# Token gates as one rounded product per token, with two pairs of PSUM banks, and the gated units unpaired

## Chip, core and metric

One NeuronCore of a Trainium2 chip runs the whole program. The metric is the device time of one execution in microseconds; before the change the median of three runs is 1869.54 us (1869.54 to 1873.31).

## What is computed

The program is a transformer of two blocks for 256 tokens of width 1024, in float32. The change lies in the last part of the second block, a retrieval of single-neuron experts. Each token has 8 heads, each head picks 16 of 128 x 128 = 16,384 experts, and each picked expert has a gate (a softmax over the 16 scores):

```
experts, gates = top 16 per head of s1[i1] + s2[i2], expert = i1 * 128 + i2
u = u_tab[ec]
a = gelu(einsum('td,thkd->thk', hc, u))
out = einsum('thk,thkd->td', gc * a, v_tab[ec])
```

The kernel does not gather. It computes h . u for all 16,384 experts and all tokens, applies gelu, multiplies by a dense matrix of gates that is zero for the experts not picked, and multiplies the result with the whole of v_tab.

## The kernel before

SyncE streams the weights through a ring of four units of 128 x 1024 floats. Float32 accuracy is had by splitting: ScalarE rounds a unit to fp32r (`ring_hi`, `unit_hi`, L489), GpSimd or VectorE computes the rest (`ring_lo`, `unit_lo`, L495), and TensorE adds the three products hi x hi, hi x lo and lo x hi. Every engine has its own queue, worked off in the order in which the code issues it, and they meet only in semaphores: `full[b]` says that TensorE has filled PSUM bank b, `emptied[b]` that it may be filled again.

The stage "peer_u" has 128 units, one per value of i2. A unit gives a tile of 128 experts (i1, on the partitions) x 256 tokens, in bank 4 or 5 in turn. There are two ways to compute it. `h_tile` (L541) issues 24 matmuls of 256 columns (L550). `h_pair_tile` (L557) puts the high and low part of h side by side as 512 columns: 8 matmuls of 512 (L562) and 8 of 256 (L568), after which the two halves of the bank must be added.

The first 44 units (`h_tile`) run while VectorE still searches the top 16. Then it hands over three rows per token: i1, i2 and the gate, 128 picks on the partitions, 256 tokens in the free dimension. From there on the 84 *gated* units run, and between them the gates are made, in 64 groups of four tokens, four groups in five units. For a token, the 128 x 128 gate matrix is the product of two one-hot matrices over the 128 picks: `hot1` (pick x i1) and `hot2` (pick x i2, multiplied by the gate). So before unit k, for its group g:

- VectorE (`one_hots`) makes `hot2` and `hot1` for four tokens with two comparisons against an iota row in PSUM and multiplies `hot2` by the gate (L2727, L2728, L2730). There are two buffers, one in the tile `late`, one over unused constants in `cst`; group g+2 is made when group g has been multiplied.
- TensorE (`token_gates`, L1264) computes four f32 products of 128 columns into one of three banks 0 to 2.
- VectorE (`gate_tokens`) multiplies the gelus of the units done so far by the gates (L2737) and copies the gates of the units to come into the places of their gelus in `act_e`, inside the tile `arena` (L2738). The n units done and the 128 - n others always make 4 x 128 elements.

For each unit VectorE adds the two halves of the pair into bank 6 or 7 (`unit_sum`, L2771), ScalarE applies gelu there (L1822; the tokens that have no gate yet go straight to `act_e`, L1824), and VectorE multiplies by the gates that are there (`gate_unit`, L2750), one unit later. After the 84 units comes the product with v_tab (L615).

Of the kernel before, what the change touches and what calls it, by code (L numbers as in the profile page):

```python
# [25 lines left out]
ALU = mybir.AluOpType  # L26
# [3 lines left out]
P = 128  # L30
# [18 lines left out]
HOT_BANKS = 3  # L49
# [163 lines left out]
def build(nc, stream, x_t, x_rows, ctx_t, params, consts, decay, lam_in, rel_bias, onehot, dist_mask, scale_w, aside_w, c_rows, ln_rows,  # L213
          bias_rows, gate_cols, out):
    with ExitStack() as ctx:
# [11 lines left out]
        def sem(name):  # L227
            return ctx.enter_context(nc.semaphore(name))
# [27 lines left out]
        gate_r = rounded("gate_r", "gate_lo", [P, T])  # L256
        e_pair = rounded("e_pair", "late", [P, 4, 2 * T], 2048)
# [33 lines left out]
        def h_parts(like, skip):  # L291
# [70 lines left out]
        hot1, hot2 = ([a[:, at:at + 4 * P].rearrange("p (t e) -> p t e", t=4) for a, at in places] for places in (  # L362
            ((late, 2048), (cst, CONST["cos_2d"])), ((late, 3072), (cst, CONST["mean_64"]))))
# [22 lines left out]
        iota_ps = ps[:, 3, 0:P]  # L386
        gate_ps = ps[:, 3, P:P + T]
# [7 lines left out]
        iota16_ps = ps[:, 7, 0:TOPK]  # L395

# [78 lines left out]
        unit_gelu = sem("unit_gelu")  # L475
# [25 lines left out]
        def _(pe):  # L501
# [733 lines left out]
            def peer_u_pair(n):  # L1235
                h_pair_tile(FIRST_UNIT["peer_u"] + n, h_parts_3, h_hi_3, 4 + n % 2)

# [20 lines left out]
            def token_gates(g):  # L1258

                b = g % HOT_BANKS  # L1260
                pe.wait_ge(hot_ready, g + 1)
                start_fill(b)
                for t in range(4):
                    m = pe.matmul(ps[:, b, t * P:(t + 1) * P], hot1[g % 2][:, t, :], hot2[g % 2][:, t, :], start=True, stop=True)  # L1264
                m.then_inc(full[b], 1)
                fills[b].add()

            for k in range(GATED_UNITS):
                for g in groups_before(k):
                    token_gates(g)  # L1270
                peer_u_pair(FIRST_GATED + k)
# [36 lines left out]
        def _(act):  # L1308
# [506 lines left out]
            for k in range(GATED_UNITS):  # L1815
                n = FIRST_GATED + k
                b = 4 + n % 2
                t = tokens_gated(k)
                unit_hi(act, FIRST_UNIT["peer_u"] + n + 2)
                act.wait_ge(emptied[b], drains[b].add())  # L1820
                total = ps[:, 6 + k % 2, 0:T]
                m = act.activation(total[:, 0:t], total[:, 0:t], ACT.Gelu)  # L1822
                if t < T:
                    m = act.activation(act_e[:, n, t:T], total[:, t:T], ACT.Gelu)  # L1824
                m.then_inc(unit_gelu, 1)
                if k >= GATED_UNITS - 3:
                    expert_hi(k - (GATED_UNITS - 3))
# [14 lines left out]
        def _(dve):  # L1842
# [877 lines left out]

            def one_hots(g):

                def of_tokens(a):
                    return a[:, 4 * g:4 * g + 4].unsqueeze(2).broadcast_to([P, 4, P])

                iotas = spread(iota_ps, 4)
                step(dve.tensor_tensor(hot2[g % 2], iotas, of_tokens(i2_t), ALU.is_equal))  # L2727
                dve.tensor_tensor(hot1[g % 2], iotas, of_tokens(i1_t), ALU.is_equal)  # L2728
                settle()
                dve.tensor_tensor(hot2[g % 2], hot2[g % 2], of_tokens(gate_ps), ALU.mult).then_inc(hot_ready, 1)  # L2730

            def gate_tokens(g, units):

                b = g % HOT_BANKS
                gates = ps[:, b, :].rearrange("p (t e) -> p e t", t=4)
                a = act_e[:, :, 4 * g:4 * g + 4]
                dve.tensor_tensor(a[:, 0:units], a[:, 0:units], gates[:, 0:units], ALU.mult)  # L2737
                dve.tensor_copy(a[:, units:N_EXP], gates[:, units:N_EXP]).then_inc(emptied[b], 1)  # L2738
# [4 lines left out]
            def gate_unit(k):  # L2743

                n = FIRST_GATED + k
                t = tokens_gated(k)
                dve.wait_ge(unit_gelu, k + 1)
                last_group = t // 4 - 1
                dve.wait_ge(emptied[last_group % HOT_BANKS], reads[last_group % HOT_BANKS].n)
                dve.tensor_tensor(act_e[:, n, 0:t], ps[:, 6 + k % 2, 0:t], act_e[:, n, 0:t],  # L2750
                                  ALU.mult).then_inc(unit_gated, 1)

            for g in range(2):
                one_hots(g)
# [11 lines left out]
            def unit_sum(k):  # L2766

                n = FIRST_GATED + k
                b = 4 + n % 2
                dve.wait_ge(full[b], n_u[n % 2].add())  # L2770
                dve.tensor_reduce(ps[:, 6 + k % 2, 0:T], ps[:, b, :].rearrange("p (a t) -> p t a", a=2), AX_X,  # L2771
                                  ALU.add).then_inc(emptied[b], 1)

            for k in range(GATED_UNITS):
                for g in groups_before(k):
                    filled(g % HOT_BANKS)
                    if g + 2 < GROUPS:
                        one_hots(g + 2)
                    if k >= 1:
                        dve.wait_ge(unit_gelu, k)  # L2780
                    gate_tokens(g, FIRST_GATED + k)
                if k >= 1:
# [4 lines left out]
            gate_unit(GATED_UNITS - 1)  # L2787
# [294 lines left out]
```

## Time and profile before

| | |
|---|---|
| median of three runs | 1869.54 us |
| the profiled execution, its own time | 1871.33 us |
| its span in the profile | 1869.5 us |
| TensorE busy | 97% |
| VectorE / GpSimd / ScalarE busy | 68% / 53% / 46% |
| granted TensorE clock, mean | 0.99 |

The busy share of TensorE is a sum over instructions that overlap, with modelled ends; how much time they really take is read from the distance between starts. The gated stage runs from 1224.0 us (first token product) to 1516.7 (first product of experts). A tile is named as the trace names it: `ps` is PSUM, `h_span` the split h, `late`, `cst` and `arena` are tiles in SBUF.

### The profile page before, as it was taken

How to read it: one execution, taken by the hardware profiler on the slowest of the kernel's cores; microseconds unless marked ns; L12 is line 12 of the kernel's file. 1: busy time of each engine (PE TensorE's matmuls, PEld its weight loads, DVE VectorE, ACT ScalarE, POOL GpSimd, SP SyncE). 2: the span in 40 equal slices, each digit the busy share in tenths (PEclk: the TensorE clock that was granted, in tenths of full speed). 3: DMA queues.
4: the chain of work that ended last, by engine and by line, in shares of the span. 5: the costliest groups of instructions: out<-in, count | busy, mean ns of one | idle time of the engine just before them, and what ended most of it. 6: DMA issues, size and time to landing. Idle time of an engine off the chain costs nothing.

```text
span 1869.5 us, 29721 instructions
## 1 busy us (share of the span) xinstructions
PE 1809.0 (97%) x10462; PEld 1528.3 (82%) x10462; DVE 1265.2 (68%) x2109; ACT 850.7 (46%) x1379; POOL 998.1 (53%) x431
## 2 busy tenths in 40 slices
PE   5999889998999999999999999999999999999999
PEld 1847579987978887788978899989988988888887
DVE  6587757888548777433233379978888867777776
ACT  3033545445445554542453546643343345554454
POOL 4034046443675543775438768876666654444443
PEclk7999999999999999999999999999999999999999
DMA  8787236886665554552325455544444455555555
GB/s 321 254 305 254 76 126 235 283 275 216 205 212 176 189 189 160 176 167 102 114 90 170 158 180 180 181 148 149 154 147 148 156 181 192 192 196 194 191 191 168
DMA packets 95316, 345.93 MB, mean 185 GB/s; under 512 B 10544, under 2 KB 12032, under 8 KB 94592
## 3 DMA queue, kind: packets, MB, share of 16 engines
q1 hardware_dynamic: 78048, 283.67, 45.1%
q10 hardware_dynamic: 17184, 61.11, 9.4%
q8 instruction: 56, 0.92, 0.2%
q14 instruction: 28, 0.23, 0.0%
HBM read 343.66 MB, written 1.08 MB: 184 GB/s over the span
## 4 chain that ended last, share of the span: by engine, by line
PE 87%; DVE 5%; DMA 3%; ACT 2%; POOL 1%; issue 1%; ACTq 0%; DVEq 0%; SPq 0%
PE ps L615 29%; PE ps L550 18%; PE ps L562 14%; PE ps L568 7%; PE ps L1264 3%; PE ps L771 2%; PE ps L534 2%; PE ps L685 2%; PE ps L838 2%; DMA ring<-stream 2%; PE ps L1001 1%; POOL ring_lo L495 1%; PE ps L785 1%; DMA cst<-consts 1%; PE ps L595 1%
## 5 line engine op out<-in xcount | busy, mean ns | idle before, releaser
L495 POOL TENSOR_TENSOR ring_lo<-ring,ring_hi 128x1024 fp32r<-128x1024 f32 x371 | 898.0, 2426 | 683.0 <-ACT ring_hi L489 681.5
L489 ACT ACTIVATE ring_hi<-ring 128x1024 fp32r<-128x1024 f32 x502 | 531.7, 1060 | 487.3 <-DMA ring<-stream 483.4
L562 PE MATMUL ps<-h_span,ring_hi 128*128 128x512 f32 x1120 | 286.0, 397 | 0.0
L550 PE MATMUL ps<-h_span,ring_hi 128*128 128x256 f32 x1952 | 258.1, 285 | 0.1
L615 PE MATMUL ps<-ring_hi,e_pair 128*128 128x512 f32 x1024 | 253.7, 389 | 1.0 <-DVE e_pair L2761 1.0
L550 PEld LDWEIGHTS ps<-h_span,ring_hi 128*128 128x128 f32 x1952 | 245.3, 192 | 5.7 <-issue 3.1
L2761 DVE TENSOR_TENSOR e_pair<-arena,e_pair 128x256 fp32r<-128x256 f32 x128 | 174.8, 1367 | 99.7 <-ACT e_pair L1813 99.3
L562 PEld LDWEIGHTS ps<-h_span,ring_hi 128*128 128x128 f32 x1120 | 202.6, 189 | 38.1
L615 PEld LDWEIGHTS ps<-ring_hi,e_pair 128*128 128x128 f32 x1024 | 192.0, 188 | 41.2 <-issue 1.4
L495 DVE TENSOR_TENSOR ring_lo<-ring,ring_hi 128x1024 fp32r<-128x1024 f32 x141 | 176.6, 1253 | 37.2 <-ACT ring_hi L489 36.9
L615 PE MATMUL ps<-ring_hi,arena_r 128*128 128x512 f32 x672 | 175.6, 394 | 2.3 <-ACT ring_hi L489 2.3
L568 PEld LDWEIGHTS ps<-h_span,ring_lo 128*128 128x128 f32 x1120 | 152.6, 190 | 11.8 <-POOL ring_lo L495 0.3
L568 PE MATMUL ps<-h_span,ring_lo 128*128 128x256 f32 x1120 | 156.0, 282 | 0.0
L2368 DVE CAST arena_r<-arena 128x256 fp32r<-128x256 f32 x64 | 105.2, 1644 | 70.0 <-ACT arena L1634 35.2
L615 PEld LDWEIGHTS ps<-ring_hi,arena_r 128*128 128x128 f32 x672 | 123.0, 190 | 26.4 <-ACT ring_hi L489 2.8
L550 PE MATMUL ps<-h_span,ring_lo 128*128 128x256 f32 x976 | 137.9, 284 | 0.3 <-POOL ring_lo L495 0.3
L615 PE MATMUL ps<-ring_lo,e_pair 128*128 128x512 f32 x512 | 137.5, 389 | 0.0
L550 PEld LDWEIGHTS ps<-h_span,ring_lo 128*128 128x128 f32 x976 | 126.7, 193 | 0.7 <-POOL ring_lo L495 0.7
L615 PEld LDWEIGHTS ps<-ring_lo,e_pair 128*128 128x128 f32 x512 | 96.1, 188 | 20.0
L1822 ACT ACTIVATE ps<-ps 128x256 f32<-128x256 f32 (+39 forms) x84 | 22.7, 270 | 173.3 <-DVE ps L2771 173.3
L615 PE MATMUL ps<-ring_lo,arena_r 128*128 128x512 f32 x320 | 91.8, 394 | 5.0 <-POOL ring_lo L495 2.8
L2352 DVE TENSOR_REDUCE arena<-ps 128x256 f32<-128x512 f32 x56 | 38.5, 687 | 65.6 <-PE ps L568 65.6
(292 smaller groups left out, 2249.4 us busy)
## 6 DMA issues: line engine op xcount, KB each, us to landing
ring<-stream SPq DMA_DIRECT2D x540, 512.0 KB, 3.3
arena<-aside_w ACTq DMA_DIRECT2D x49, 512.0 KB, 4.7
late<-aside_w ACTq DMA_DIRECT2D x21, 512.0 KB, 4.6
resid<-aside_w ACTq DMA_DIRECT2D x10, 512.0 KB, 6.4
arena<-scale_w ACTq DMA_DIRECT2D x8, 512.0 KB, 15.5
arena<-ln_rows ACTq DMA_DIRECT2D x8, 512.0 KB, 5.0
arena<-gate_cols ACTq DMA_DIRECT2D x2, 1024.0 KB, 5.0
arena<-decay ACTq DMA_DIRECT2D x1, 1536.0 KB, 6.8
```

The costliest lines, as they stand in the source:

```text
L489: act.activation(ring_hi[:, s, :], ring[:, s, :], ACT.Copy).then_inc(hi_ready, 1)
L495: eng.tensor_tensor(ring_lo[:, s, :], ring[:, s, :], ring_hi[:, s, :], ALU.subtract).then_inc(lo_ready[s], 1)
L534: m = pe.matmul(ps[:, bank, at:at + n], w[:, kc * P:(kc + 1) * P], r, start=kc == 0, stop=kc == KC - 1)
L550: m = pe.matmul(ps[:, bank, 0:T], w[:, kc * P:(kc + 1) * P], x[:, kc, :], start=begin, stop=w is w_lo and kc == KC - 1)
L562: m = pe.matmul(ps[:, bank, :], w_hi[:, kc * P:(kc + 1) * P], parts[kc], start=kc == 0, stop=False, skip_group_check=True)
L568: m = pe.matmul(ps[:, bank, 0:T], w_lo[:, kc * P:(kc + 1) * P], h_hi[:, kc, :], start=False, stop=kc == KC - 1, skip_group_check=True)
L615: m = pe.matmul(ps[:, b, :], x[:, tt * P:(tt + 1) * P], w[:, half * 512:(half + 1) * 512], start=start, stop=stop, skip_group_check=True)
L685: pe.matmul(shape, lhs, rhs, start=True, stop=True).then_inc(full[bank], 1)
L1264: m = pe.matmul(ps[:, b, t * P:(t + 1) * P], hot1[g % 2][:, t, :], hot2[g % 2][:, t, :], start=True, stop=True)
L2352: dve.tensor_reduce(dst, ps[:, b, :].rearrange("p (a t) -> p t a", a=2), AX_X, ALU.add).then_inc(emptied[b], 1)
L2368: dve.tensor_copy(hid_hi[:, j % 4, :], hid2[:, j % 4, :]).then_inc(hid_hi_ready, 1)
L2761: dve.tensor_tensor(e_lo[:, e % 4, :], act_e[:, e if row is None else row, :], e_hi[:, e % 4, :], ALU.subtract).then_inc(e_lo_ready, 1)
```

## The change

The gates are now split like everything else. The gate is rounded to fp32r (`gate_hi`), the rest is `gate_lo`, and VectorE makes a `hot2` of 256 columns per token, hi part and lo part side by side, both fp32r; TensorE multiplies it in one fp32r matmul of 256 columns. A group of four tokens now fills two banks, 0 and 1 or 2 and 3, in turn. The two halves of the result have to be added: ScalarE copies the hi half out of PSUM (for the n units done to one of two new buffers `gate_part`, for the others into `act_e`), and VectorE adds the lo half to both and then multiplies the first sum by the gelus. The gated units go through `h_tile` instead of `h_pair_tile`, so their sum is complete in bank 4 or 5, `unit_sum` goes, gelu reads that bank and writes to bank 6, and `gate_unit` comes in the same turn of the loop. Iota and gates move to bank 7, the gates for half of the tokens at a time.

```
-HOT_BANKS = 3
+HOT_BANKS = ((0, 1), (2, 3))
...
             def token_gates(g):
-                b = g % HOT_BANKS
                 pe.wait_ge(hot_ready, g + 1)
-                start_fill(b)
-                for t in range(4):
-                    m = pe.matmul(ps[:, b, t * P:(t + 1) * P], hot1[g % 2][:, t, :], hot2[g % 2][:, t, :], start=True, stop=True)
-                m.then_inc(full[b], 1)
-                fills[b].add()
+                for first, b in zip((0, 2), HOT_BANKS[g % 2]):
+                    start_fill(b)
+                    for t in range(2):
+                        m = pe.matmul(ps[:, b, t * T:(t + 1) * T], hot1[g % 2][:, first + t, :],
+                                      hot2_parts[g % 2][:, first + t, :], start=True, stop=True)
+                    m.then_inc(full[b], 1)
+                    fills[b].add()
...
-                peer_u_pair(FIRST_GATED + k)
+                peer_u_tile(FIRST_GATED + k)
...
                 unit_hi(act, FIRST_UNIT["peer_u"] + n + 2)
-                act.wait_ge(emptied[b], drains[b].add())
-                total = ps[:, 6 + k % 2, 0:T]
-                m = act.activation(total[:, 0:t], total[:, 0:t], ACT.Gelu)
+                for g in groups_before(k):
+                    low, high = HOT_BANKS[g % 2]
+                    act.wait_ge(full[low], mark["group", g][low])
+                    act.wait_ge(full[high], mark["group", g][high])
+                    if g >= 2:
+                        act.wait_ge(emptied[low], mark["group", g - 2][low])
+                    hi, _, tokens, part = group_parts(g)
+                    act.activation(part[:, 0:n], hi[:, 0:n], ACT.Copy)
+                    act.activation(tokens[:, n:N_EXP], hi[:, n:N_EXP], ACT.Copy).then_inc(group_copied, 1)
+                act.wait_ge(full[b], drains[b].add())
+                if k >= 1:
+                    act.wait_ge(unit_gated, k)
+                m = act.activation(gelu_ps[k % 2][:, 0:t], ps[:, b, 0:t], ACT.Gelu)
                 if t < T:
-                    m = act.activation(act_e[:, n, t:T], total[:, t:T], ACT.Gelu)
-                m.then_inc(unit_gelu, 1)
+                    m = act.activation(act_e[:, n, t:T], ps[:, b, t:T], ACT.Gelu)
+                m.then_inc(emptied[b], 1)
...
-            step(dve.tensor_copy(gate_hi[:, :], ps[:, 6, 0:T]))
+            step(dve.tensor_copy(gate_r[:, :], ps[:, 6, 0:T]))
             settle()
-            dve.tensor_copy(gate_ps, gate_hi[:, :]).then_inc(emptied[6], 1)
+            step(dve.tensor_copy(gate_hi[:, :], gate_r[:, :]))
+            settle()
+            dve.tensor_tensor(gate_lo[:, :], ps[:, 6, 0:T], gate_hi[:, :], ALU.subtract).then_inc(emptied[6], 1)
...
+            def half_gates(tt):
+                c = slice(tt * P, (tt + 1) * P)
+                dve.tensor_copy(gate_hi_ps, gate_hi[:, c])
+                step(dve.tensor_copy(gate_lo_ps, gate_lo[:, c]))
...
-                step(dve.tensor_tensor(hot2[g % 2], iotas, of_tokens(i2_t), ALU.is_equal))
-                dve.tensor_tensor(hot1[g % 2], iotas, of_tokens(i1_t), ALU.is_equal)
+                hi, lo = hot2_parts[g % 2][:, :, 0:P], hot2_parts[g % 2][:, :, P:2 * P]
+                step(dve.tensor_tensor(hi, iotas, of_tokens(i2_t), ALU.is_equal))
+                dve.tensor_tensor(hot1[g % 2][:, :, :], iotas, of_tokens(i1_t), ALU.is_equal)
                 settle()
-                dve.tensor_tensor(hot2[g % 2], hot2[g % 2], of_tokens(gate_ps), ALU.mult).then_inc(hot_ready, 1)
+                dve.tensor_tensor(lo, hi, of_tokens(gate_lo_ps, 4 * g % P), ALU.mult)
+                dve.tensor_tensor(hi, hi, of_tokens(gate_hi_ps, 4 * g % P), ALU.mult).then_inc(hot_ready, 1)
...
-                dve.tensor_tensor(a[:, 0:units], a[:, 0:units], gates[:, 0:units], ALU.mult)
-                dve.tensor_copy(a[:, units:N_EXP], gates[:, units:N_EXP]).then_inc(emptied[b], 1)
+                low, high = HOT_BANKS[g % 2]
+                dve.wait_ge(group_copied, g + 1)
+                hi, lo, a, part = group_parts(g)
+                step(dve.tensor_tensor(hi[:, 0:units], lo[:, 0:units], part[:, 0:units], ALU.add))
+                dve.tensor_tensor(a[:, units:N_EXP], lo[:, units:N_EXP], a[:, units:N_EXP], ALU.add)
+                settle()
+                dve.tensor_tensor(a[:, 0:units], hi[:, 0:units], a[:, 0:units], ALU.mult).then_inc(emptied[low], 1)
+                dve.wait_ge(emptied[low], mark["group", g][low])
+                dve.sem_inc(emptied[high], 1)
...
             for k in range(GATED_UNITS):
                 for g in groups_before(k):
...
-                if k >= 1:
-                    gate_unit(k - 1)
-                unit_sum(k)
+                gate_unit(k)
```

On TensorE, this is the second group and the second gated unit, before the change (`hot_ready` counts one-hots made; an f32 product stands here as one instruction and in the trace as two):

```order
L1264 MATMUL ps<-cst 128x128 [waits emptied1,hot_ready]
L1264 MATMUL ps<-cst 128x128 x3
L562 MATMUL ps<-h_span_52,ring_hi 128x512 [waits emptied5,hi_ready]
L562 MATMUL ps<-h_span_52,ring_hi 128x512 x7
L568 MATMUL ps<-h_span_52,ring_lo_49 128x256 [waits lo_ready1]
L568 MATMUL ps<-h_span_52,ring_lo_49 128x256 x7
```

and with it:

```order
L1270 MATMUL ps<-hot2_parts_b_55,hot1_b_57 128x256 [waits emptied2,hot_ready]
L1270 MATMUL ps<-hot2_parts_b_55,hot1_b_57 128x256
L1270 MATMUL ps<-hot2_parts_b_55,hot1_b_57 128x256 [waits emptied3]
L1270 MATMUL ps<-hot2_parts_b_55,hot1_b_57 128x256
L559 MATMUL ps<-h_span_52,ring_hi 128x256 [waits emptied5,hi_ready]
L559 MATMUL ps<-h_span_52,ring_hi 128x256 x15
L559 MATMUL ps<-h_span_52,ring_lo_49 128x256 [waits lo_ready1]
L559 MATMUL ps<-h_span_52,ring_lo_49 128x256 x7
```

The four products wait for two banks instead of one and are twice as wide; the unit's 8 + 8 matmuls have become 24.

On VectorE, one turn of the loop with a group, before the change: the one-hots, the gates of the tokens, the gated unit of the turn before, the sum of the halves.

```order
L2727 TENSOR_TENSOR cst<-ps,late 128x512 [waits full1]
L2728 TENSOR_TENSOR cst<-ps,late 128x512
L2730 TENSOR_TENSOR cst<-cst,ps 128x512 [waits dve_step]
L2737 TENSOR_TENSOR arena<-arena,ps 128x45x4 [waits unit_gelu]
L2738 COPY arena<-ps 128x83x4
L2750 TENSOR_TENSOR arena<-ps,arena 128x4 [waits emptied0,unit_gelu]
L2771 TENSOR_REDUCE ps<-ps 128x256 [waits full5]
```

and with it:

```order
L2754 TENSOR_TENSOR hot2_parts_b_55<-ps,late 128x4x128 [waits full3,full2]
L2755 TENSOR_TENSOR hot1_b_57<-ps,late 128x512
L2757 TENSOR_TENSOR hot2_parts_b_55<-hot2_parts_b_55,ps 128x4x128 [waits dve_step]
L2758 TENSOR_TENSOR hot2_parts_b_55<-hot2_parts_b_55,ps 128x4x128
L2765 TENSOR_TENSOR ps<-ps,gate_part_b 128x45x4 [waits group_copied]
L2766 TENSOR_TENSOR arena<-ps,arena 128x83x4
L2768 TENSOR_TENSOR arena<-ps,arena 128x45x4 [waits dve_step]
L2783 TENSOR_TENSOR arena<-ps,arena 128x8 [waits emptied2,emptied5]
```

`hot2_parts_b` and `hot1_b` are the second buffer of one-hots. There is a fourth operation on the one-hots, the copy has become an addition and one more addition stands ahead of the multiply, which waits for the first addition (`dve_step`). The wait for ScalarE's copies (`group_copied`) is new. The row of `gate_unit` now ends the turn of its own unit, waiting for that unit's gelu (`emptied5`), and the reduce is gone.

On VectorE ahead of the first group, from the last of the three handed-over rows to the first one-hots, before the change:

```order
L2713 COPY gate_hi<-ps 128x256 [waits full6]
L2715 COPY ps<-gate_hi 128x256 [waits dve_step]
L2717 COPY ps<-cst 128x128 [waits emptied7]
L2727 TENSOR_TENSOR late<-ps,late 128x512 [waits emptied6,iota_ready]
L2728 TENSOR_TENSOR late<-ps,late 128x512
L2730 TENSOR_TENSOR late<-late,ps 128x512 [waits dve_step]
```

and with it:

```order
L2731 CAST gate_r_53<-ps 128x256 [waits full6]
L2733 CAST gate_hi<-gate_r_53 128x256 [waits dve_step]
L2735 TENSOR_TENSOR gate_lo<-ps,gate_hi 128x256 [waits dve_step]
L2737 COPY ps<-cst 128x128 [waits emptied7]
L2744 COPY ps<-gate_hi 128x128 [waits emptied6,iota_ready]
L2745 COPY ps<-gate_lo 128x128
L2754 TENSOR_TENSOR hot2_parts_a_54<-ps,late 128x4x128 [waits dve_step]
L2755 TENSOR_TENSOR hot1_a_56<-ps,late 128x512
L2757 TENSOR_TENSOR hot2_parts_a_54<-hot2_parts_a_54,ps 128x4x128 [waits dve_step]
L2758 TENSOR_TENSOR hot2_parts_a_54<-hot2_parts_a_54,ps 128x4x128
```

A cast and a subtraction are new, and the gates are copied to PSUM as two halves of 128 columns, ahead of four instead of three operations on the one-hots.

## Rows read from the trace of the kernel before

**Rows 1.** The page: busy us (share of span) of each engine; TensorE clock in slices.

```profile
PE 1809.0 (97%) x10462; PEld 1528.3 (82%) x10462; DVE 1265.2 (68%) x2109; ACT 850.7 (46%) x1379; POOL 998.1 (53%) x431
...
PEclk7999999999999999999999999999999999999999
```

**Rows 2.** Busy us (x instructions) of each engine in the gated stage.

```profile
1224.00:1516.70 292.70, 292.70 (x1858) 263.30 (x1857) 237.42 (x482) 117.02 (x248) 197.26 (x83) 1.00 0.46 151
```

**Rows 3.** Timeline of TensorE: start us, us, engine, line, operation, tiles, count.

```profile
1302.62 2.09 PE L562 MATMUL ps<-h_span,ring_hi 128*128 128x512 f32 x8
...
1305.50 1.05 PE L1264 MATMUL ps<-cst 128*128 128x128 f32 x8
1306.31 0.96 PE L562 MATMUL ps<-h_span,ring_hi 128*128 128x512 f32 x3
```

**Rows 4.** Timeline of TensorE at the end of the stage, units without a group.

```profile
1505.53 2.00 PE L562 MATMUL ps<-h_span,ring_hi 128*128 128x512 f32 x8
...
1508.32 2.00 PE L562 MATMUL ps<-h_span,ring_hi 128*128 128x512 f32 x8
```

**Rows 5.** Timeline of TensorE in the stage just before, unpaired units.

```profile
1193.55 2.08 PE L550 MATMUL ps<-h_span,ring_hi 128*128 128x256 f32 x16
...
1196.43 2.08 PE L550 MATMUL ps<-h_span,ring_hi 128*128 128x256 f32 x16
```

**Rows 6.** Timeline of VectorE beside rows 3.

```profile
1302.90 0.69 DVE L2727 TENSOR_TENSOR late<-ps,late 128x512 f32<-128x512 f32 x1 [0.19 <-PE ps L1264]
1303.51 0.68 DVE L2728 TENSOR_TENSOR late<-ps,late 128x512 f32<-128x512 f32 x1
1304.11 0.68 DVE L2730 TENSOR_TENSOR late<-late,ps 128x512 f32<-128x512 f32 x1
1304.70 0.42 DVE L2737 TENSOR_TENSOR arena<-arena,ps 128x264 f32<-128x264 f32 x1
1305.04 0.41 DVE L2738 COPY arena<-ps 128x248 f32<-128x248 f32 x1
1305.37 0.22 DVE L2750 TENSOR_TENSOR arena<-ps,arena 128x72 f32<-128x72 f32 x1
1305.70 0.70 DVE L2771 TENSOR_REDUCE ps<-ps 128x256 f32<-128x512 f32 x1
```

**Rows 7.** Timeline of VectorE late in the stage.

```profile
1490.83 0.65 DVE L2737 TENSOR_TENSOR arena<-arena,ps 128x476 f32<-128x476 f32 x1
1491.39 0.19 DVE L2738 COPY arena<-ps 128x36 f32<-128x36 f32 x1
1491.49 0.40 DVE L2750 TENSOR_TENSOR arena<-ps,arena 128x240 f32<-128x240 f32 x1
```

**Rows 8.** Timeline of ScalarE beside rows 3, and the split behind the gelu.

```profile
1302.74 0.21 ACT L1822 ACTIVATE ps<-ps 128x72 f32<-128x72 f32 x1 [2.32 <-DVE ps L2771]
1302.87 0.32 ACT L1824 ACTIVATE arena<-ps 128x184 f32<-128x184 f32 x1
1303.07 1.06 ACT L489 ACTIVATE ring_hi<-ring 128x1024 fp32r<-128x1024 f32 x1
```

**Rows 9.** Timeline of VectorE before the first group.

```profile
1214.61 2.31 DVE L2706 TENSOR_TENSOR cst<-cst,small 128x128 f32<-128x128 f32 x1
...
1218.48 0.42 DVE L2713 COPY gate_hi<-ps 128x256 f32<-128x256 f32 x1 [0.20 <-PE ps L1251]
1218.93 0.43 DVE L2715 COPY ps<-gate_hi 128x256 f32<-128x256 f32 x1
...
1220.80 0.68 DVE L2730 TENSOR_TENSOR late<-late,ps 128x512 f32<-128x512 f32 x1
```

**Rows 10.** Timeline of GpSimd over the same stretch.

```profile
1214.36 2.41 POOL L495 TENSOR_TENSOR ring_lo<-ring,ring_hi 128x1024 fp32r<-128x1024 f32 x1 [2.08 <-ACT ring_hi L489]
1217.00 4.76 POOL L495 TENSOR_TENSOR ring_lo<-ring,ring_hi 128x1024 fp32r<-128x1024 f32 x2 [0.23 <-ACT ring_hi L489]
```

**Rows 11.** Timeline of TensorE at the first group.

```profile
1224.04 1.06 PE L1264 MATMUL ps<-late 128*128 128x128 f32 x8
```

More of the change, by code:

```diff
@@ L256, in build @@
         gate_r = rounded("gate_r", "gate_lo", [P, T])
+        hot2_parts = [rounded("hot2_parts_a", "late", [P, 4, 2 * P], 2048), rounded("hot2_parts_b", "cst", [P, 4, 2 * P], CONST["cos_2d"])]
+        hot1 = [rounded("hot1_a", "late", [P, 4, P], 3072), rounded("hot1_b", "cst", [P, 4, P], CONST["mean_64"])]
+        gate_part = [sb("gate_part_a", [P, N_EXP - 4, 4]), sb("gate_part_b", [P, N_EXP - 4, 4])]
         e_pair = rounded("e_pair", "late", [P, 4, 2 * T], 2048)
@@ L395, in build, with group_parts @@
         iota16_ps = ps[:, 7, 0:TOPK]
+        gelu_ps = [ps[:, 6, 0:T], ps[:, 6, T:2 * T]]
+        def group_parts(g):
+            low = HOT_BANKS[g % 2][0]
+            parts = ps[:, low:low + 2, :].rearrange("p b (t a e) -> p e (b t) a", t=2, a=2)
+            return parts[:, :, :, 0], parts[:, :, :, 1], act_e[:, :, 4 * g:4 * g + 4], gate_part[g % 2]
         landed = [sem(f"landed{s}") for s in range(RING)]
@@ L1258, in token_gates @@
             def token_gates(g):
-                b = g % HOT_BANKS
                 pe.wait_ge(hot_ready, g + 1)
-                start_fill(b)
-                for t in range(4):
-                    m = pe.matmul(ps[:, b, t * P:(t + 1) * P], hot1[g % 2][:, t, :], hot2[g % 2][:, t, :], start=True, stop=True)
-                m.then_inc(full[b], 1)
-                fills[b].add()
+                for first, b in zip((0, 2), HOT_BANKS[g % 2]):
[5 more added lines that the diff above has]
+                    fills[b].add()
+                mark["group", g] = [fills[b].n for b in range(4)]
             for k in range(GATED_UNITS):
@@ L2764, in expert_lo @@
                     unit_lo(dve, FIRST_UNIT["peer_v"] + e, i)
[L2766 to L2772, printed above, removed]
             for k in range(GATED_UNITS):
                 for g in groups_before(k):
-                    filled(g % HOT_BANKS)
+                    for b in HOT_BANKS[g % 2]:
+                        dve.wait_ge(full[b], mark["group", g][b])
+                    if g + 2 == GROUPS // 2:
+                        half_gates(1)
+                        settle()
                     if g + 2 < GROUPS:
                         one_hots(g + 2)
-                    if k >= 1:
-                        dve.wait_ge(unit_gelu, k)
                     gate_tokens(g, FIRST_GATED + k)
-                if k >= 1:
-                    gate_unit(k - 1)
-                unit_sum(k)
+                gate_unit(k)
                 if k >= GATED_UNITS - 3:
                     expert_lo(k - (GATED_UNITS - 3))
-            gate_unit(GATED_UNITS - 1)
             for e in range(3, 8):
```

26 lines of the change are left out of this document (11 added, 15 removed).

## Prediction

> **What bounds the kernel now.** I read the engine table first: TensorE is busy for 97% of the span and the granted clock stands at its 2.4 GHz level in every slice but the first [rows 1]. A reader should then ask which stage the change touches and whether TensorE has any idle time there. The table of windows, cut at the first and the last matmul of the gated stage, answers both: 292.7 us, TensorE busy in all of them, VectorE for 237.4, ScalarE for 117.0, GpSimd for 197.3, DMA under half [rows 2]. No engine makes TensorE wait there, so an edit that takes TensorE time out of this stage gives it back one for one, until another engine needs more than what is left. That engine would be VectorE, at 81% now.
>
> The timeline gives the stage's rhythm. A unit with a group of token gates comes round every 1306.31 - 1302.62 = 3.69 us [rows 3], one without a group every 1508.32 - 1505.53 = 2.79 [rows 4]. So a group costs 0.90 us of TensorE, although its own starts are only 0.81 apart: the first matmuls behind it come a little later. 64 groups and 84 units give 64 x 3.69 + 20 x 2.79 = 292.0, against 292.7 measured. The model holds.
>
> **TensorE, the token products.** An f32 product of 128 columns stands in the trace as two instructions, eight per group of four tokens, 0.90 / 8 = 0.11 us each. After the change a token is one rounded matmul of 256 columns. The stage just before has hundreds of these, with the same kind of weight load: 24 of them from 1193.55 to 1196.43, that is 2.88 us, 0.120 each [rows 5]. A group becomes 4 x 0.120 = 0.48. Gain 0.42 x 64 = 26.9 us. Bounds for one product: below, 0.101, the distance of the starts of one f32 instruction now ((1306.31 - 1305.50) / 8), which would bring 4.9 us more; above, the 0.225 that a token costs now, which would take back all 26.9. I take 0.120, the row of the same shape.
>
> **TensorE, units unpaired.** 16 matmuls (8 of 512, 8 of 256 columns) become 24 of 256. The paired unit costs 2.79, the unpaired 2.88 [rows 4, 5], both on weights out of the same ring and the same h. Cost 0.09 x 84 = 7.6 us. Nothing has to be guessed here.
>
> So TensorE alone needs 84 x 2.88 + 64 x 0.48 = 272.6 us for the stage: 20.0 less than the 292.7. In five units (four with a group) it needs 5 x 2.88 + 4 x 0.48 = 16.32 instead of 4 x 3.69 + 2.79 = 17.55.
>
> **VectorE, the edit's price.** Per group now: three operations of 512 elements, 0.60 us from start to start, then 0.34 and 0.33 for the multiply and the copy, and per unit the 0.60 reduce and the multiply of the gated unit [rows 6]. After: four of the 512 kind (2.40), two additions which together always have 512 elements (0.34 + 0.33 = 0.67), a multiply of 4n elements, a wait for that multiply's own end, a semaphore increment, and the unit's multiply. The multiply costs 0.34 at n = 66 [rows 6] and 0.56 at n = 119 [rows 7]. Its own end comes 0.65 - 0.56 = 0.09 after the next could have started, plus 0.03 to go on (0.42 us from 1218.48, next at 1218.93) [rows 9]; the increment I estimate at 0.05, since no row shows one. The unit's multiply is 0.22 long at 72 elements and 0.40 at 240 [rows 6, 7], less the 0.07 by which the next one overlaps it: 0.15 and 0.33. Sum for a unit with a group, D: 2.40 + 0.67 + 0.34 + 0.17 + 0.15 = 3.73 at n = 66 and 2.40 + 0.67 + 0.56 + 0.17 + 0.33 = 4.13 at n = 119. The reduce is gone; the unit without a group costs VectorE 0.33.
>
> VectorE keeps pace while 4 D + 0.33 is under 16.32, so while D is under 4.00. By the line through the two values D passes it at n = 102, the 58th of the 80 units among which the groups are spread; from there to the last D is over by 0.08 on average, x 4/5 x 22 = 1.4 us in all. This is lag, not yet a stall of TensorE. VectorE frees the banks of a group about 4.6 us after the unit ahead of it ended, TensorE asks for them two groups later, after 6.72. Some 2 us of lag are covered, of which the lag inside a block of five uses part. I charge 0.5 us. This is the weakest number of the forecast: each 0.1 us more per group moves the crossing 13 units forward, and the excess grows with the square of the units behind it (1.4, 3.7, 7.0, 11 us for 0, 0.1, 0.2, 0.3 more), of which about 1 is covered. On the other side nothing is to be had: VectorE can't make TensorE faster than its own 16.32. That there are ends this far apart is why I keep B and C below.
>
> A new dependency comes with it: VectorE now ends every unit by waiting for that unit's gelu. From the end of a unit to the gelu's end lie 0.20 until another engine starts on it (TensorE goes on at 1305.50, VectorE starts at 1305.70) and 0.45 for both pieces [rows 3, 6, 8]; in units with a group VectorE arrives later anyway, in the fifth it waits and starts the next group's work 0.95 after the unit's end. That is in the 0.33 and the 16.32 above. Queued behind the wait are the one-hots of group g+2, which TensorE wants 3 us after they are due.
>
> The Trainium skill has a rule against this change. "VectorE: DVE Perf Modes", section "The DRAIN you can't avoid", says that the next operation doesn't start until the pipe of the one before is empty. By durations (0.68 instead of 0.60 for each large one, the same 0.08 for the small ones) VectorE would set the stage. Here the trace disagrees for this very mix: starts 0.60 apart at durations of 0.68 [rows 6]. But one of the new operations writes PSUM with a stride and the multiply reads what it wrote, so I keep it as a rival.
>
> **ScalarE.** It gains two copies per group, together 512 elements. The gelu pieces take 0.21 for 72 and 0.32 for 184 elements and together 0.45 from the first start to the end [rows 8]; twice the elements, by the slope of these two rows ((0.32 - 0.21) / 112 = 1 ns each), make some 0.7 for both copies. Its load becomes 5 x (1.06 + 0.45) + 4 x 0.7 = 10.4 of 16.32. The copies stand behind the 1.06 split of a ring unit, which waits for its DMA; with 0.65 for the gelu and nothing for the DMA they end 2.4 us after the unit's end, VectorE wants them at 0.95 + 2.40 = 3.35. Covered by 0.95, which a late landing may use up now and then.
>
> **Start and end of the stage.** Before the first group VectorE gains a cast and a subtraction of 256 elements, two copies of 128 and a fourth one-hot operation: 0.45 + 0.34 + 0.5 + 0.6 less the 0.34 copy that goes, 1.55 us. The one-hots of group 0 were ready at 1220.80 + 0.68 = 1221.48, while TensorE came for them at 1224.04 [rows 9, 11]. Cover 2.5. The cast reads and writes SBUF only. The row to look at is L2706: 2.31 us for 128 elements, where 256 took 0.43 at 1218.93, and it ends 0.15 after GpSimd's pass of 2.41 from 1214.36; another pair of GpSimd passes runs from 1217.00 to 1221.76, right where the cast will stand [rows 9, 10]. Held until the first of them ends (1219.4, 0.45 late), group 0 is ready at 1221.48 + 1.55 + 0.45 = 1223.5, still in time; held for both, 2.4 later, at 1225.9, 1.8 us late. I take the first. (The Trainium skill, "GPSIMD Engine Reference", section "Specifications", says that the SBUF interfaces are shared with VectorE, and that an operation in a 2-port mode or with two SBUF inputs contends. By that rule, the trace agrees.) At the stage's end VectorE leaves one unit earlier than now; TensorE hardly waits there today, so nothing.
>
> **Sum.** 26.9 - 7.6 = 19.3 by the parts, 20.0 by the stage (292.7 - 272.6; the 0.7 is what the rhythm model leaves out, half of it taken); less 0.5 for the lag and nothing for the start: 19.2. Against the profiled execution, span 1869.5 and its own time 1871.33, that is a span of 1850.3 and 1852.1. The median of the runs, 1869.54, lies 1.8 under the profiled one, and my forecast is for the median: 1850.3.
>
> **Rivals.**
> A, the forecast: TensorE bounds, 1850 (1847 to 1853). 68%.
> B, VectorE falls behind in part: 0.1 to 0.3 us more per group than I sum, from strided PSUM writes, the wait on its own multiply and the increment, or copies of ScalarE that come late. For 0.2 more: 7.0 - 1 = 6 lost instead of 0.5, 1855.8; for 0.3: 10 lost, 1860. For it: VectorE is filled to (64 x 3.86 + 20 x 0.33) / 272.6 = 93%; against: every operand shape but the PSUM-written sum has a row. 19%.
> C, VectorE sets the stage, the slower side: every operation of a group costs its duration, 7 x 0.08 = 0.56 more. D is then 3.86 + 0.56 = 4.42 on average over n = 44 to 123, and the excess 64 x 0.42 = 27, less 1 covered, against 19.7 gained: 1876. It decides from a mean D of 4.32 on (64 x 0.32 = 20.5), 0.46 above mine. 8%.
> D, the product is not cheaper: 256 columns with one-hots as the loaded weights cost the 0.225 per token of now, so only the unpairing is left, +7.6: 1877. The rows of 256 columns speak against it. 3%.
> Between B and C lies a strip in which gain and loss cancel to within 3.7 us. 2%.
>
> A difference below 0.2% (3.7 us) can't be told from no change. Faster: A + B = 0.87; same 0.02; slower C + D = 0.11. The range must hold 0.8: all of A and most of B, 1847 to 1862; the lower end takes in a product somewhat under 0.120.
>
> **What would show it.** The stage from the first token product to the first expert product takes 273 us instead of 292.7; a group's starts lie 0.48 apart and a unit's 2.88; TensorE stays at 99 to 100% busy there. VectorE's busy share of the stage rises above 90%. If B, TensorE shows idle time before a token product or the unit behind it, put down to VectorE, in the last third of the stage and not in the first; if C, in all of it; if D, matmuls of 256 columns 0.2 us apart with TensorE still full. A late first group would show as idle time of 1 to 2 us at 1224. The forecast is wrong if TensorE is full and the stage still isn't 17 us shorter.

## Result and the profile after

| | before | with the change |
|---|---|---|
| median of 8 runs each | 1874.13 us (1869.54 to 1880.07) | 1862.92 us (1858.26 to 1867.15) |
| ratio, 95% interval | 1 | 0.9932 (0.9914 to 0.9950) |
| the profiled execution, span | 1869.5 | 1856.2 |
| gated stage, first token product to first product of experts | 292.7 | 279.9 |
| the rest of the span | 1576.9 | 1576.3 |

The ratio stands for 12.7 us less (9.3 to 16.1); the profiled executions differ by 13.3, of which the gated stage holds 12.8. The forecast was 19.2 less. The forecast was written for 1869.54, the median of the first three of the eight runs of the kernel before; the median of all eight is 1874.13. Applied to 1869.54, the ratio gives 1856.8 (1853.5 to 1860.2): inside the range of 1847 to 1862, 6.5 above the forecast, and outside the 1847 to 1853 of its main case. A second measurement of the same kernel, beside the experiments below, gave 0.9952 (0.9934 to 0.9970).

The stage in the table of windows, columns as in [rows 2]:

```profile
1223.66:1503.54 279.88, 274.75 (x2274) 272.67 (x2273) 246.75 (x531) 156.97 (x376) 199.45 (x84) 1.00 0.48 159
```

TensorE was busy without a gap before; now it lacks 5.1 us, and VectorE is busy for 88% of a shorter stage. On TensorE the early part of the stage has this rhythm (timeline):

```profile
1305.00 0.64 PE L1270 MATMUL ps<-hot_parts_a,hot_a 128*128 128x256 f32 x4
1305.48 2.08 PE L559 MATMUL ps<-h_span,ring_hi 128*128 128x256 f32 x16
1307.40 1.12 PE L559 MATMUL ps<-h_span,ring_lo 128*128 128x256 f32 x8
1308.36 0.63 PE L1270 MATMUL ps<-hot_parts_b,hot_b 128*128 128x256 f32 x4
```

A group is 1305.48 - 1305.00 = 0.48 us and a unit 1308.36 - 1305.48 = 2.88, against the 3.69 for both in [rows 3]. Late in the stage the token products come late:

```profile
1477.36 0.63 PE L1270 MATMUL ps<-hot_parts_b,hot_b 128*128 128x256 f32 x4
1477.82 2.07 PE L559 MATMUL ps<-h_span,ring_hi 128*128 128x256 f32 x16
1479.73 1.12 PE L559 MATMUL ps<-h_span,ring_lo 128*128 128x256 f32 x8
1481.44 0.71 PE L1270 MATMUL ps<-hot_parts_a,hot_a 128*128 128x256 f32 x4 [0.59 <-DVE arena L2768]
1481.99 2.08 PE L559 MATMUL ps<-h_span,ring_hi 128*128 128x256 f32 x16
...
1485.72 0.71 PE L1270 MATMUL ps<-hot_parts_b,hot_b 128*128 128x256 f32 x4 [0.70 <-DVE arena L2768]
```

From 1477.82 to 1481.99 the unit with its group takes 4.17 instead of 3.36, so 0.81 are lost, of which the wait shown is 0.59; that is why ten waits of 5.0 us go with a stage that is some 8 us too long. The wait before the product is put down to the multiply L2768 of VectorE, which frees the banks. The table of waits of the stage (who waited for whom: us, times, longest) adds the same wait as seen from the weight load, ScalarE's waits for VectorE, and VectorE's waits for itself and for ScalarE:

```profile
ACT ps L1840 <- DVE arena L2783: 65.1, 33, 2.9
...
DVE arena L2783 <- DVE arena L2768: 14.1, 64, 0.6
DVE arena L2783 <- ACT ps L1840: 9.7, 5, 2.5
DVE arena L2783 <- ACT arena L1842: 9.2, 15, 1.0
PEld ps L1270 <- issue: 7.0, 11, 0.9
PE ps L1270 <- DVE arena L2768: 5.0, 10, 0.7
```

All ten waits of TensorE lie behind 1380 us, so from the 49th of the 84 gated units on. The five waits of 9.7 us stand in the last five units, after the groups; the 15 of 9.2 us stand in the units without a group before those, twelve of them 0.57 long. (The changed kernel's lines are numbered anew: L1270 is the token product, L559 the unit; the trace calls `hot2_parts_a` and `hot1_a` `hot_parts_a` and `hot_a`.) What VectorE does in a turn, early (timeline, n = 45):

```profile
1228.88 0.69 DVE L2754 TENSOR_TENSOR hot_parts_b<-ps,late 128x512 fp32r<-128x512 f32 x1
...
1231.95 0.33 DVE L2768 TENSOR_TENSOR arena<-ps,arena 128x180 f32<-128x180 f32 x1
1232.49 0.17 DVE L2783 TENSOR_TENSOR arena<-ps,arena 128x8 f32<-128x8 f32 x1 [0.21 <-DVE arena L2768]
1232.60 0.69 DVE L2754 TENSOR_TENSOR hot_parts_a<-ps,late 128x512 fp32r<-128x512 f32 x1
```

and late (n = 117), in the last turn of a block of five with a group and the fifth without one, with ScalarE's gelu of the fifth unit under it:

```profile
1472.33 0.68 DVE L2754 TENSOR_TENSOR hot_parts_b<-ps,late 128x512 fp32r<-128x512 f32 x1
...
1474.71 0.65 DVE L2765 TENSOR_TENSOR ps<-ps,gate_part_b 128x468 f32<-128x468 f32 x1
1475.27 0.19 DVE L2766 TENSOR_TENSOR arena<-ps,arena 128x44 f32<-128x44 f32 x1
1475.40 0.65 DVE L2768 TENSOR_TENSOR arena<-ps,arena 128x468 f32<-128x468 f32 x1
1476.26 0.41 DVE L2783 TENSOR_TENSOR arena<-ps,arena 128x240 f32<-128x240 f32 x1 [0.21 <-DVE arena L2768]
1477.24 0.41 DVE L2783 TENSOR_TENSOR arena<-ps,arena 128x240 f32<-128x240 f32 x1 [0.57 <-ACT arena L1842]
1477.56 0.68 DVE L2754 TENSOR_TENSOR hot_parts_a<-ps,late 128x512 fp32r<-128x512 f32 x1
```

```profile
1476.76 0.35 ACT L1840 ACTIVATE ps<-ps 128x240 f32<-128x240 f32 x1 [2.86 <-DVE arena L2783]
1477.03 0.18 ACT L1842 ACTIVATE arena<-ps 128x16 f32<-128x16 f32 x1
```

Early a turn costs 1232.60 - 1228.88 = 3.72 us. Late it costs 1476.26 + 0.32 - 1472.33 = 4.25 (0.32 is what the unit's multiply takes from start to start, 1477.24 to 1477.56). Between the multiply L2768 and the unit's multiply L2783 lie 0.21 us in which VectorE waits for its own last result. And in the fifth unit VectorE stands still for 0.57 until ScalarE's gelu is done, although the unit was finished long before: that gelu had itself waited for VectorE's multiply of the unit before.

Ahead of the first group VectorE's rows now read, answering to [rows 9]:

```profile
1218.57 0.60 DVE L2733 COPY gate_hi<-gate_r 128x256 f32<-128x256 f32 x1
1219.21 0.42 DVE L2735 TENSOR_TENSOR gate_lo<-ps,gate_hi 128x256 f32<-128x256 f32 x1
1219.55 0.28 DVE L2737 COPY ps<-cst 128x128 f32<-128x128 f32 x1
...
1222.19 0.68 DVE L2758 TENSOR_TENSOR hot_parts_a<-hot_parts_a,ps 128x512 fp32r<-128x512 f32 x1
```

The cast between two SBUF tiles is L2733. GpSimd ran here too (4.79 us for two passes from 1216.64, the first of them over at about 1219.04), and the cast lasted until 1219.17, 0.60 us for 256 elements where the subtraction behind it took 0.42. That fits a cast held until GpSimd's first pass ended; no run takes GpSimd away to show it. The first one-hots were ready at 1222.87, TensorE came at 1223.66. Nothing was lost.

### The profile page after: what moved, and what is told of

Same layout as the page of the kernel before. It is cut to its first block, busy times and chain, and to the rows that moved or that the text cites. A ratio compares the mean times of both kernels' runs of the same rounds, so it can differ in the third digit from the quotient of the medians.

```text
span 1856.2 us, 31003 instructions
## 1 busy us (share of the span) xinstructions
PE 1790.4 (96%) x10878; PEld 1537.8 (83%) x10878; DVE 1275.7 (69%) x2158; ACT 889.7 (48%) x1507; POOL 1004.1 (54%) x431
## 4 chain that ended last, share of the span: by engine, by line
PE 70%; DVE 14%; issue 6%; POOL 4%; DMA 3%; ACT 2%; DVEq 0%; ACTq 0%; POOLq 0%; SPq 0%
PE ps L624 26%; PE ps L559 19%; PE ps L571 5%; POOL ring_lo L504 4%; PE ps L577 3%; PE ps L780 2%; PE ps L543 2%; DMA ring<-stream 2%; PE ps L847 2%; PE ps L694 2%; PE ps L1010 2%; PE ps L794 1%; DVE arena L2768 1%; DVE ps L2765 1%; DMA cst<-consts 1%
## 5 line engine op out<-in xcount | busy, mean ns | idle before, releaser
L559 PE MATMUL ps<-h_span,ring_hi 128*128 128x256 f32 x3296 | 431.8, 284 | 0.0
L559 PEld LDWEIGHTS ps<-h_span,ring_hi 128*128 128x128 f32 x3296 | 411.4, 191 | 5.4 <-issue 3.3
L559 PE MATMUL ps<-h_span,ring_lo 128*128 128x256 f32 x1648 | 231.4, 283 | 0.8 <-POOL ring_lo L504 0.7
L559 PEld LDWEIGHTS ps<-h_span,ring_lo 128*128 128x128 f32 x1648 | 212.5, 192 | 1.5 <-POOL ring_lo L504 1.5
L571 PE MATMUL ps<-h_span,ring_hi 128*128 128x512 f32 x448 | 111.4, 391 | 0.0
L571 PEld LDWEIGHTS ps<-h_span,ring_hi 128*128 128x128 f32 x448 | 82.3, 188 | 16.0
L1354 ACT ACTIVATE arena<-ps 128x256 f32<-128x256 f32 (+2 forms) x90 | 34.7, 387 | 101.1 <-PE ps L559 89.5
L624 PEld LDWEIGHTS ps<-ring_lo,arena_r 128*128 128x128 f32 x320 | 59.8, 190 | 19.9 <-POOL ring_lo L504 4.5
```

The costliest lines, as they stand in the source:

```text
L559: m = pe.matmul(ps[:, bank, 0:T], w[:, kc * P:(kc + 1) * P], x[:, kc, :], start=begin, stop=w is w_lo and kc == KC - 1)
L571: m = pe.matmul(ps[:, bank, :], w_hi[:, kc * P:(kc + 1) * P], parts[kc], start=kc == 0, stop=False, skip_group_check=True)
L624: m = pe.matmul(ps[:, b, :], x[:, tt * P:(tt + 1) * P], w[:, half * 512:(half + 1) * 512], start=start, stop=stop, skip_group_check=True)
```

## Experiments

Stage lengths are those of each kernel's profiled execution, from the first token product to the first product of experts; span less stage is everything else, which no experiment touches. It lies between 1575.6 and 1584.2 (the changed kernel alone: 1576.3 and 1584.2), so the small steps are read from the stage and the ratio only confirms them.

| kernel | stage | rest | ratio to before, 95% interval |
|---|---|---|---|
| the kernel before | 292.7 | 1576.9 | 1 |
| changed | 279.9 | 1576.3 | 0.9932 (0.9914 to 0.9950) |
| changed, once more | 280.4 | 1584.2 | 0.9952 (0.9934 to 0.9970) |
| gelu in place | 276.8 | 1576.6 | 0.9923 (0.9900 to 0.9945) |
| one release | 271.8 | 1579.7 | 0.9902 (0.9880 to 0.9924) |
| both | 272.0 | 1575.6 | 0.9902 (0.9880 to 0.9925) |
| less work for VectorE | 271.8 | 1576.4 | 0.9894 (0.9851 to 0.9936) |
| more work for VectorE | 317.3 | 1580.4 | 1.0155 (1.0121 to 1.0188) |
| before, units unpaired | 298.8 | 1579.6 | 1.0030 (1.0013 to 1.0047) |

**The changed kernel again**, on the chip on which gelu in place, one release and both were measured. The other three experiments ran on a second chip, each beside the kernel before.

> The changed kernel as it is, beside the others on the same chip: stage 279.9 us, 7.6 of it idle time and late starts before token products from the 46th gated unit on, ratio to the kernel before 0.993.

The stage came out at 280.4, with 5.4 us of waits of the products and 7.7 of the weight loads ahead of them, at 11 and 13 places, the first before the 44th gated unit (1372.18 us), where the first run has its first before the 49th. The ratio was 0.9952 where 0.993 had been expected; the two intervals overlap. In the profiled execution what lies outside the stage was 7.9 us longer than in the first run. Part of it are waits of TensorE for `ring_lo` from VectorE in earlier stages, 7.0 us against 0.9; the rest is not traced.

**Less work for VectorE.**

```
-                dve.tensor_tensor(lo, hi, of_tokens(gate_lo_ps, 4 * g % P), ALU.mult)
+                if g < 2:
+                    dve.tensor_tensor(lo, hi, of_tokens(gate_lo_ps, 4 * g % P), ALU.mult)
```

> The changed kernel, but the multiplication of the one-hots by the low part of the gates is left out from the third group on (the low half keeps what an earlier group left, so the gates are wrong there). It takes 0.60 us of VectorE per group away and touches no wait, bank or transfer. Theory (VectorE's time is what TensorE waits for): D is 3.64 at most, 4 x 3.64 + 0.98 = 15.5 under 16.3, so no wait of TensorE is left, stage 272.3. Rival (copies of ScalarE, ring landings, or the bank order hold TensorE up): stage stays over 278.

```profile
1222.20:1493.98 271.78, 271.78 (x2274) 271.78 (x2273) 210.38 (x469) 161.99 (x376) 199.81 (x84) 1.00 0.49 164
```

TensorE is busy for all of 271.8 us, at the value that 84 units of 2.88 and 64 groups of 0.48 make (272.6), to 0.8. One VectorE operation less per group, with all waits, banks, copies and transfers as they were, removes all of the loss. So the loss was VectorE's time, not late copies or landings.

**More work for VectorE.**

```
                 step(dve.tensor_tensor(hi, iotas, of_tokens(i2_t), ALU.is_equal))
+                step(dve.tensor_tensor(lo, iotas, of_tokens(i2_t), ALU.is_equal))
```

> The changed kernel with one more comparison of 512 elements per group on VectorE, whose result is overwritten: 0.60 us per group more. Theory: VectorE sets the whole stage, five units take 4 x (3.98 + 0.60) + 0.98 = 19.3 on average against TensorE's 16.3, so 16 x 19.3 plus the four last units less the lag covered at the end, about 318 us; that is the slope of 0.6 us per group over the changed kernel's 280, and slower than the kernel before by some 25. Rival: a stage of under 290 would mean that VectorE was not near its limit.

The stage came out at 317.3, within a microsecond of the expectation, and the rival's 290 is out. TensorE late in the stage (timeline):

```profile
1496.29 0.63 PE L1270 MATMUL ps<-hot_parts_b,hot_b 128*128 128x256 f32 x4
1497.34 2.15 PE L559 MATMUL ps<-h_span,ring_hi 128*128 128x256 f32 x16 [0.42 <-ACT arena L1842]
...
1501.97 0.71 PE L1270 MATMUL ps<-hot_parts_a,hot_a 128*128 128x256 f32 x4 [1.52 <-DVE arena L2769]
...
1506.80 0.71 PE L1270 MATMUL ps<-hot_parts_b,hot_b 128*128 128x256 f32 x4 [1.24 <-DVE arena L2769]
```

The unit at 1497.34 waits for ScalarE's gelu to free its bank, and 62 of the gelus waited for a multiply of VectorE in this stage. 64 x 0.60 = 38.4 us more work gave 37.4 us more time. From where the kernel stands, these 38 us of VectorE cost almost as much time, while the one taken away in the experiment before gave back only 8.1 of 62 x 0.60 = 37.2: TensorE's own time is met after that.

**Gelu in place**, which takes the chain between gelu and multiply apart. In the changed kernel both gelu buffers lie in bank 6, and ScalarE waits (`unit_gated`) until VectorE has read the last before it writes the next.

```
-                if k >= 1:
-                    act.wait_ge(unit_gated, k)
-                m = act.activation(gelu_ps[k % 2][:, 0:t], ps[:, b, 0:t], ACT.Gelu)
+                m = act.activation(ps[:, b, 0:t], ps[:, b, 0:t], ACT.Gelu)
...
-                m.then_inc(emptied[b], 1)
+                m.then_inc(unit_gelu, 1)
...
-                dve.wait_ge(emptied[4 + n % 2], n_u[n % 2].add())
+                dve.wait_ge(unit_gelu, k + 1)
...
-                dve.tensor_tensor(act_e[:, n, 0:t], gelu_ps[k % 2][:, 0:t], act_e[:, n, 0:t],
-                                  ALU.mult).then_inc(unit_gated, 1)
+                dve.tensor_tensor(act_e[:, n, 0:t], ps[:, 4 + n % 2, 0:t], act_e[:, n, 0:t],
+                                  ALU.mult).then_inc(emptied[4 + n % 2], 1)
```

> The changed kernel, but gelu is applied in place in bank 4 or 5, VectorE reads it there and frees the bank, and ScalarE no longer waits for VectorE's multiply of the unit before. Theory (VectorE sets the pace late in the stage; a unit with a group costs it 3.72 us early and 4.24 late, and the fifth unit 0.98 instead of 0.33, because gelu of unit k waits for the multiply of k-1 and the multiply of k for that gelu): the fifth unit falls to about 0.35, VectorE keeps pace with TensorE's 16.3 per five units up to D = 4.0 instead of 3.83, and of the 7.6 us that the stage lasts over its 272.3 some 2 to 3 are left: stage about 275, span about 1851. Rival (ScalarE's copies or late ring landings hold VectorE up, the chain through gelu is covered by lag): stage stays at 280, within 1 us.

```profile
1467.36 0.68 DVE L2754 TENSOR_TENSOR hot_parts_b<-ps,late 128x512 fp32r<-128x512 f32 x1
...
1470.42 0.65 DVE L2768 TENSOR_TENSOR arena<-ps,arena 128x468 f32<-128x468 f32 x1
1471.28 0.72 DVE L2783 TENSOR_TENSOR arena<-ps,arena 128x240 f32<-128x240 f32 x2 [0.21 <-ACT arena L1841]
1471.92 0.68 DVE L2754 TENSOR_TENSOR hot_parts_a<-ps,late 128x512 fp32r<-128x512 f32 x1
```

The two unit multiplies now stand together (x2) and the last turn of a block with its fifth unit takes 1471.92 - 1467.36 = 4.56 instead of 1477.56 - 1472.33 = 5.23. The chain was there and cost 0.67 per block, as the theory says. The stage fell by 3.1 (3.6 beside its own repeat), to 276.8, while 5 had been expected. The waits before token products are gone. A wait of another kind took their place: VectorE now frees the unit's bank, and late in the stage TensorE waits for that, behind the first group of a block:

```profile
1470.53 0.64 PE L1271 MATMUL ps<-hot_parts_a,hot_a 128*128 128x256 f32 x4
1471.84 2.15 PE L560 MATMUL ps<-h_span,ring_hi 128*128 128x256 f32 x16 [0.67 <-DVE arena L2783]
```

There are six such waits (2.7 us) and nine of the weight load (4.4 us), and the stage is 5.0 longer than the 271.8 of a full TensorE. How much of that VectorE's excess would have cost anyway, 2 to 3 by the expectation, and how much is due to the bank that now comes free later, no run separates.

**One release.** The two banks of a group share one pair of semaphores, and the unit's multiply waits for the second addition, not for the multiply in front of it.

```
-                dve.tensor_tensor(a[:, units:N_EXP], lo[:, units:N_EXP], a[:, units:N_EXP], ALU.add)
-                settle()
+                first_sum = steps.now()
+                step(dve.tensor_tensor(a[:, units:N_EXP], lo[:, units:N_EXP], a[:, units:N_EXP], ALU.add))
+                dve.wait_ge(dve_step, first_sum)
                 dve.tensor_tensor(a[:, 0:units], hi[:, 0:units], a[:, 0:units], ALU.mult).then_inc(emptied[low], 1)
-                dve.wait_ge(emptied[low], mark["group", g][low])
-                dve.sem_inc(emptied[high], 1)
+                mark["second_sum"] = steps.now()
...
-                b = HOT_BANKS[last_group % 2][0]
-                dve.wait_ge(emptied[b], mark["group", last_group][b])
+                dve.wait_ge(dve_step, mark["second_sum"])
```

TensorE signals and waits for the low bank's semaphores alone, and so do the waits of ScalarE and VectorE.

> The changed kernel, but the two banks of a group share one pair of semaphores, so that VectorE neither waits for its own last multiply nor increments a second semaphore, and the unit's multiply waits only for the second addition. Theory: D falls by 0.22 to 0.30 us, to 3.45 early and 3.95 late; the excess never gets past the 2 us of cover; no idle time of TensorE before a token product; stage 272.5, span about 1848.7. Rival (what stalls is the order in which banks come free, two groups ahead, not VectorE's time): the release comes 0.1 us earlier only, stage 278 to 280.

```profile
1472.69 0.68 DVE L2756 TENSOR_TENSOR hot_parts_a<-ps,late 128x512 fp32r<-128x512 f32 x1
...
1475.77 0.65 DVE L2771 TENSOR_TENSOR arena<-ps,arena 128x476 f32<-128x476 f32 x1
1476.34 0.40 DVE L2783 TENSOR_TENSOR arena<-ps,arena 128x244 f32<-128x244 f32 x1
1476.66 0.68 DVE L2756 TENSOR_TENSOR hot_parts_b<-ps,late 128x512 fp32r<-128x512 f32 x1
```

```profile
1227.12:1498.91 271.79, 271.79 (x2274) 271.79 (x2273) 240.68 (x531) 161.44 (x376) 199.88 (x84) 1.00 0.49 163
```

From the multiply (1475.77) to the unit's multiply (1476.34) are 0.57 for 476 elements, with no idle time; in the changed kernel it was 0.86 for the same operation (1480.64 to 1481.50). The turn costs 3.97 where it cost 4.27 (1477.56 to 1481.83), so 0.30 less. TensorE is full, the stage 271.8. The rival's 278 to 280 is out. The edit takes two things away at once, the increment behind its wait and the wait of the unit's multiply for the multiply in front; no run takes one alone.

**Both edits.**

> Both edits of the two kernels before. Theory: VectorE needs 4 x 3.95 + 0.35 = 16.15 late in the stage, just under TensorE's 16.3; stage 272.3, not better than with one release alone by more than 0.5 us, because TensorE is full in either. Rival: if something other than VectorE's time stalls TensorE, idle time stays in the last third and the stage is over 275.

The stage was 272.0, the ratio 0.9902, and the spans of the two kernels differ only in what lies outside the stage. With TensorE full, the second edit has nothing left to give. Either of these two is the better kernel: by the ratio 18.3 us less than the 1869.54 of the kernel before (14 to 22).

**Units unpaired alone**, in the kernel before.

```
-                peer_u_pair(FIRST_GATED + k)
+                peer_u_tile(FIRST_GATED + k)
...
-                total = ps[:, 6 + k % 2, 0:T]
+                total = ps[:, b, 0:T]
...
-                if k >= 1:
-                    gate_unit(k - 1)
-                unit_sum(k)
+                gate_unit(k)
```

> The kernel before, with its f32 token products, but the gated units computed by 24 matmuls of 256 columns instead of 8 of 512 and 8 of 256, and with it no sum of halves on VectorE (gelu in place in bank 4 or 5, the unit's multiply in its own turn). It measures the unpairing by itself. Prediction's term: 0.09 us per unit, 7.6 in all, stage 292.7 + 7.6 = 300.3, TensorE full, VectorE's busy time down by 84 x 0.70 = 59. Rival: the f32 products' late following matmuls (0.09 per group) go away behind 256-column matmuls, so that it is only 2 us slower.

```profile
1302.47 2.17 PE L550 MATMUL ps<-h_span,ring_hi 128*128 128x256 f32 x16
...
1305.43 1.05 PE L1264 MATMUL ps<-late 128*128 128x128 f32 x8
1306.24 2.16 PE L550 MATMUL ps<-h_span,ring_hi 128*128 128x256 f32 x16
```

A unit with a group takes 3.77 us where it took 3.69, one without 2.88 where it took 2.79: 64 x 0.08 + 20 x 0.09 = 6.9; the stage grew by 6.1 and the ratio says 5.6 (2.4 to 8.8). The prediction's 7.6 was somewhat high, because it took 0.09 for all 84 units. The rival's 2 us is out: behind 256-column matmuls a group still costs 3.77 - 2.88 = 0.89. VectorE's busy time in the stage fell from 237.4 to 186.8, so by 50.6 instead of 59. What remains between this kernel and the changed one with a full TensorE is the token product alone: 298.8 - 271.8 = 27.0.

## Why the prediction was partly right

**Which engine bounds.** Right for the kernel before: TensorE had no gap there, and time taken from it came back until VectorE's limit was met. With VectorE out of the way all of it comes back: 292.7 - 271.8 = 20.9, which is 27.0 less 6.1.

**The token product: 26.9 less.** Right. It measured 27.0, and 0.48 per group.

**The unpairing: 7.6 more.** Right in kind and 1.5 too high, 6.1 measured. By these two TensorE's own stage was put at 272.6; with no wait in the way it is 271.8 to 272.0.

**VectorE's excess: 0.5 charged.** This is the step that failed, by its size. 279.9 - 271.8 = 8.1 us were lost where 0.5 were charged, so 12.8 were left of the 20.9. The mechanism was named, with the crossing and the growth with the square, and so was the case: what came about is rival B, given 19%, and not the forecast A, given 68%. The stated range held because most of B had been taken into it. Two durations were too small:

- The wait for the multiply's own end and the increment were summed to 0.17. From L2768 to L2783 late in the stage it is 0.86 us, of which 468 elements take 0.56 (as from L2765 to L2766): 0.30. It makes D 3.72 at n = 45 (the prediction's line gives 3.57) and 4.25 at n = 117 (it gives 4.12).
- The fifth unit was put at 0.33. When VectorE lags, it is 0.98, since gelu and multiply of neighbouring units wait for each other. The prediction saw that VectorE waits for the gelu; it did not follow the gelu's own wait, `unit_gated`, back to VectorE. The limit for D falls from 4.00 to (16.32 - 0.98) / 4 = 3.84.

With these two the prediction's own formula crosses at n = 61 instead of 102 and finds an excess of 0.8 x 62 x 0.23 = 11.4 us, less some 2 covered (an estimate, from the prediction): 9.4, against the 8.1 measured. That is somewhat high for two reasons: the last two groups make no new one-hots, and 0.98 is the late value of the fifth unit, which cost 0.85 at n = 78 (next one-hots at 1338.97, the multiply before it started at 1337.93 and takes 0.19 from start to start). A third thing works the other way: the gates of the second half of the tokens are copied to PSUM in the middle of the stage, 0.51 us of VectorE before the one-hots at 1347.36. The prediction counted these two copies only for the first half, ahead of the stage. Taking either duration away shortens the turn, or the block, as the two experiments show; with the first gone TensorE is full and the stage 271.8, with the second gone the stage is shorter by 3.1.

**The rule that operations cost their full duration** (rival C) did not hold: the starts of the four large operations stay 0.60 apart at durations of 0.68, the addition that writes PSUM takes 0.56 from start to start at 468 elements and is 0.65 long, like the multiply that writes SBUF ([rows 7], 476 elements). **Rival D** (no cheaper product) is out by the 0.48. **ScalarE's copies** were covered: in the changed kernel one wait for them of 0.3 us was left in the whole stage. **The start** went as described: the cast ended 0.13 us after the first of GpSimd's passes and not after the second, and the one-hots were ready with 0.8 us to spare. **Where the loss shows** was right in kind: in waits before a token product, none before the 49th unit, which is 56% of the way through the stage and so earlier than its last third. VectorE's busy share did not rise above 90%: it was 88%, since the time in which it waits for its own result (14.1 us) or for a gelu (18.9 us) is not busy.

## What to carry to other kernels

When an edit loads a second engine almost as much as the bounding one (93% by the prediction's sum here), charge the waits between its own operations as carefully as the operations, and follow each new wait to the end: if A waits for B and B's work waits for A's last, the pair costs a full round trip as soon as one of them lags. Look for an engine that waits for its own result only to signal a second semaphore: one signal for things that are freed together, with the next wait moved back by one operation, took 0.30 us off a late group here and all of the loss from the stage. A plain test of the bound is to take one operation off the suspected engine and to add one: here -8.1 and +37.4 us for some 38 us of work either way, which says that the engine bounds, and how far down the next bound lies.

## What the runs showed of the hardware

An operation of VectorE that waits for the one in front of it went on 0.03 us after that one's end ([rows 9], 1218.48 to 1218.93: 0.45 from start to start). Operations of the same 256 elements and the same length of 0.42 stand 0.34 apart where the second does not wait for the first (1219.21 to 1219.55 in the changed kernel), so such a wait cost 0.11. With a semaphore increment standing between the two as an instruction of its own, behind its own wait, the idle time was 0.21 us in the rows shown and 14.1 us in the 64 groups together. The prediction had allowed 0.03 for the wait and 0.05 for the increment, beside 0.09 for the overlap.

Runs of one kernel lie up to 0.8% apart (1858.26 to 1867.15 for the changed one, 1858.91 to 1873.60 beside the experiments), and the rest of the span outside the stage differed by 7.9 us between the two profiled executions of the changed kernel, while its stage repeated within 0.5 us (279.9 and 280.4). A change inside a stage is therefore better told from the stage than from the total.
